# A two-layer transformer trunk on one core: FFN second product of groups 0 to 7 as Strassen's seven block products, with weight block sums on GpSimd

## The reference, cut to what matters

```python
def conv_ffn(x, w_in, conv_w, conv_b, w_out):
    up, gate = jnp.split(x @ w_in, 2, axis=-1)          # x 256x1024, w_in 1024x5632
    up = conv1d_causal_depthwise(up, conv_w) + conv_b   # 3 taps along the tokens
    return (jax.nn.gelu(up) * gate) @ w_out             # hidden 256x2816, w_out 2816x1024
...
x = layer_norm(DEEPNORM_ALPHA * x + conv_ffn(x, ...), ln_g[layer, 1], ln_b[layer, 1])
```

## Time and profile before

| | |
|---|---|
| median of 3 runs | 592.69 us |
| the profiled execution's own time | 593.44 us |
| its span (first to last instruction) | 590.9 us |
| PE busy | 580.6 us (98%) |
| weight loads of PE (beside matmuls) | 473.7 us (80%) |
| VectorE busy | 448.5 us (76%) |
| ScalarE busy | 335.3 us (57%) |
| GpSimd busy | 50.9 us (9%) |
| mean granted TensorE clock | 0.997 |
| DMA | 127.86 MB, mean 216 GB/s |

### The profile page before, as it was taken

How to read it: one execution, slowest core, us unless ns; L and a number is a source line. 1 busy time by engine, 2 the same in 40 slices (tenths; PEclk the granted TensorE clock), 3 DMA queues, 4 the chain that set the end, 5 groups by cost and what they waited for, 6 DMA issues and landing times.

```text
span 590.9 us, 7752 instructions
## 1 busy us (share of the span) xinstructions
PE 580.6 (98%) x2720; PEld 473.7 (80%) x2720; DVE 448.5 (76%) x813; ACT 335.3 (57%) x560; POOL 50.9 (9%) x84
## 2 busy tenths in 40 slices
PE   8999999999999999999999999999999999999995
PEld 6887777788888888888888888887888888888884
DVE  4889995886688777667879796778677888766656
ACT  4767584245566656554545678944556574555530
POOL 5300000400000000000120003132000000000003
PEclk9999999999999999999999999999999999999998
DMA  8997876456668798866456955442965889777511
GB/s 298 297 325 232 273 176 214 132 182 207 202 211 262 252 336 259 262 207 219 154 202 192 333 175 174 136 143 72 311 184 181 252 257 334 243 235 246 179 36 71
DMA packets 95665, 127.86 MB, mean 216 GB/s; under 512 B 13404, under 2 KB 73612, under 8 KB 95628
## 3 DMA queue, kind: packets, MB, share of 16 engines
q1 hardware_dynamic: 94188, 123.19, 65.3%
q0 software_dynamic: 1152, 4.19, 2.0%
q10 hardware_dynamic: 288, 0.00, 0.0%
HBM read 108.23 MB, written 1.05 MB: 185 GB/s over the span
## 4 chain that ended last, share of the span: by engine, by line
PE 95%; DVE 3%; DMA 1%; ACT 0%; issue 0%; SPq 0%; DVEq 0%
PE wide L1288 18%; PE wide L1290 17%; PE wide L1289 17%; PE score L1290 6%; PE score L1288 6%; PE score L1289 6%; PE outb L1290 3%; PE turn L1290 3%; PE outb L1288 3%; PE turn L1288 3%; PE outb L1289 3%; PE turn L1289 3%; DMA xs<-in_x 1%; DVE xT L994 1%; PE turn L1387 1%; PE outb L1413 1%
## 5 line engine op out<-in xcount | busy, mean ns | idle before, releaser
L977 DVE TENSOR_TENSOR w_lo<-raw,w_hi 128x2048 fp32r<-128x2048 f32 (+1 forms) x120 | 210.5, 1776 | 60.5 <-ACT w_hi L790 60.3
L790 ACT ACTIVATE w_hi<-raw 128x2048 fp32r<-128x2048 f32 (+1 forms) x126 | 184.2, 1488 | 92.3 <-PE wide L1290 45.5
L1288 PE MATMUL wide<-w_hi,oT_hi 128*128 128x512 f32 x240 | 95.0, 396 | 0.0
L1290 PE MATMUL wide<-w_hi,oT_lo 128*128 128x512 f32 x240 | 93.5, 390 | 0.0
L1289 PE MATMUL wide<-w_lo,oT_hi 128*128 128x512 f32 x240 | 93.5, 390 | 0.0
L1288 PE MATMUL wide<-w_hi,xT 128*128 128x512 f32 x224 | 89.9, 401 | 0.5 <-DVE xT L994 0.3
L1290 PE MATMUL wide<-w_hi,xT 128*128 128x512 f32 x224 | 87.4, 390 | 0.0
L1289 PE MATMUL wide<-w_lo,xT 128*128 128x512 f32 x224 | 87.3, 390 | 0.0
L1288 PE MATMUL score<-w_hi,xT 128*128 128x512 f32 x160 | 62.2, 389 | 0.0
L1289 PE MATMUL score<-w_lo,xT 128*128 128x512 f32 x160 | 62.2, 389 | 0.0
L1290 PE MATMUL score<-w_hi,xT 128*128 128x512 f32 x160 | 62.2, 389 | 0.0
(11 more groups left out here) (160 smaller groups left out, 837.9 us busy)
## 6 DMA issues: line engine op xcount, KB each, us to landing
raw<-in_ffn_w_in SPq DMA_DIRECT2D x88, 512.0 KB, 5.4
raw<-in_ffn_w_out SPq DMA_DIRECT2D x22, 1024.0 KB, 7.6
kT<-turned SPq DMA_DIRECT2D x104, 128.0 KB, 2.8
raw<-in_a_w_qkv SPq DMA_DIRECT2D x9, 1024.0 KB, 6.8
raw<-in_w_kv_shared SPq DMA_DIRECT2D x8, 1024.0 KB, 7.0
raw<-in_a_w_o SPq DMA_DIRECT2D x4, 1024.0 KB, 6.2
raw<-in_b_w_q SPq DMA_DIRECT2D x4, 1024.0 KB, 5.1
raw<-in_b_w_o SPq DMA_DIRECT2D x4, 1024.0 KB, 5.2
```

Source lines behind the costliest of these rows:

```text
L790: ins = nc.scalar.activation(w_hi[c % RING][:, part], raw[c % RAW_RING][:, part], ACT.Copy)
L977: ins = nc.vector.tensor_tensor(w_lo[c % RING][:, part], raw[c % RAW_RING][:, part], w_hi[c % RING][:, part].bitcast(F32), ALU.subtract)
L1288: nc.tensor.matmul(dst, a_hi, b_hi, start=start, stop=False, skip_group_check=True)
L1290: return nc.tensor.matmul(dst, a_lo, b_hi, start=False, stop=stop, skip_group_check=True)
```

## The change

**Second product of groups 0 to 7** (`FOLDED = 8`). The 2x2 blocks are: hidden, by token tile and feature tile; weights, by feature tile and half of the output columns. Instead of eight block products there are seven, each of one 128x128 stationary operand and 512 moving columns (21 matmuls a group instead of 24), of sums and differences of blocks:
- hidden side: `combine` (DVE) makes five sums into `h_sums` (three instructions), then hi and lo of 5 + 2 tiles.
- weight side, a chunk of 2048 columns becomes 3584: the two plain blocks (`fold_plain_hi` on ACT, `fold_plain_lo` on DVE, 1024 columns), and five sums. GpSimd's `fold_weights` makes the sums (1024, 1024 and 512 columns), ACT their hi parts (1024 and 1536), GpSimd the lo parts (1024 and 1536). These results have one buffer each (`fold_hi`/`fold_lo`, parts a and b).
- the seven products accumulate over the eight groups in seven PSUM banks: four in part A (`fold_a`), three in part B (`fold_b`). So one bank, `side[3]`, is left for the first products of groups 2 to 9, and both token tiles use it in turn.
- after group 7 VectorE adds the seven banks to the residual, 12 instructions of 128x512 (`add_folded`), before groups 8 to 10 use `wide`.

**PE's order** is now, for group i: first product of token tile 0 (24 matmuls), part A of group i-2 (12), first product of token tile 1 (24), part B of group i-2 (9).

**The last group's first product** (`in_features`) has the weights stationary and the 256 tokens moving: 96 matmuls of 256 columns instead of 48 of 512. Its result has the features on the partitions, so its transposes and move fall away (`MOVES = GROUPS - 1`).

**Chunks of groups 8 and 9** of w_out are split by GpSimd (four instructions of 1024 columns a layer). Some buffers change place so that the new ones fit.

The core of the diff:

```diff
-HIDDEN = 4
-MOVE_AHEAD = 6
+FOLDED = 8
...
+        POOL_SPLITS[2 * layer, 1] = ([], [(c + 2 * GROUPS + n, half) for n in range(2) for half in range(2)])
...
+        fold_a = ((1, wide[0]), (0, side[0]), (2, side[2]), (3, side[1]))
+        fold_b = ((6, wide[1]), (5, wide[3]), (4, wide[2]))
...
+            def fold_weights(t):
+                four = quadrants(t)
+                pool.wait_ge(raw_in[raw_slot("fold", t)], raw_count("fold", t))
+                if t:
+                    pool.wait_ge(sum_lo_done, t)
+                nc.gpsimd.tensor_tensor(fold_sums[0].rearrange("p (t n) -> p t n", t=2), four[:, :, 0, :], four[:, :, 1, :],
+                                        ALU.add).then_inc(sums_a_done, 1)
+                if t:
+                    pool.wait_ge(fold_b_lo_done, t)
+                nc.gpsimd.tensor_tensor(fold_sums[1][:, 0:D].rearrange("p (h n) -> p h n", h=2), four[:, 1, :, :], four[:, 0, :, :],
+                                        ALU.subtract)
+                nc.gpsimd.tensor_tensor(fold_sums[1][:, D:D + HALF], four[:, 0, 0, :], four[:, 1, 1, :],
+                                        ALU.add).then_inc(sums_b_done, 1)
+                pool.wait_ge(sum_hi_done, t + 1)
+                nc.gpsimd.tensor_tensor(fold_lo[0][:, CHUNK // 2:CHUNK], fold_sums[0], fold_hi[0][:, CHUNK // 2:CHUNK].bitcast(F32),
+                                        ALU.subtract).then_inc(sum_lo_done, 1)
+                pool.wait_ge(fold_b_hi_done, t + 1)
+                nc.gpsimd.tensor_tensor(fold_lo[1], fold_sums[1], fold_hi[1].bitcast(F32),
+                                        ALU.subtract).then_inc(fold_b_lo_done, 1)
...
+                def out_folded(j, half):
+                    t, b = FOLDED * layer + j, j % 2
+                    if half == 0:
+                        pe.wait_ge(hlo_done, 2 * (GROUPS * layer + j) + 2)
+                        pe.wait_ge(plain_lo_done, t + 1)
...
+                    else:
+                        pe.wait_ge(fold_b_lo_done, t + 1)
+                    for n, (tile, bank) in enumerate(fold_b if half else fold_a):
+                        if half == 0 and n == 2:
+                            pe.wait_ge(sum_lo_done, t + 1)
...
+                for i in range(MOVES):
+                    for st in range(ST):
+                        in_half(i, st)
+                        if i >= 2:
+                            out_folded(i - 2, st)
+                for which in range(2):
+                    in_features(which)
```

More of the change, by code:

```diff
@@ L328, in yoco_trunk @@
             POOL_SPLITS[2 * layer + 1, 0] = ([], [(c + 1, 1), (c + 2, 0)])
-    POOL_PARTS = [part for n in range(2 * LAYERS) for st in range(ST) for parts in POOL_SPLITS.get((n, st), ([], [])) for part in parts]
+    for n in range(2 * LAYERS):
+        for st in range(ST):
+            for parts in POOL_SPLITS.get((n, st), ([], [])):
+                POOL_PARTS += parts
     POOL_CHUNKS = sorted({c for c, _ in POOL_PARTS})
@@ L629, in _ @@
                         else:
[L630 removed]
+                            load("chunk", c, (lambda r: r.rearrange("p (k n) -> p k n", k=4), src))
                         if c == FIRST + 2:
@@ L643, in load_in @@
                     for h in range(2):
-                        load(ffn_chunk(layer, i, h),
+                        load("chunk", in_chunk(layer, i, h),
                              *[(lambda r, w=w: r.rearrange("p (k w n) -> p k w n", k=4, w=2)[:, :, w, :],
@@ L938, in _ @@
+                    if 1 <= i <= FOLDED:
+                        fold_b_hi(i - 1)
+                    if i < GROUPS - 1:
+                        split_hi(in_chunk(layer, i, 1) + RING)
+                make_h_hi(GROUPS - 1)
+                for c in (base + LAYER_CHUNKS, base + LAYER_CHUNKS + 1):
+                    for half in range(2):
+                        split_hi(c, half)
                 if layer + 1 < LAYERS:
@@ new lines, in turn_in @@
+                    dve.wait_ge(*((in_rows_done, u + 1) if st == 0 else (chunk_used, in_chunk(layer, i, 1) + 1)))
+                    if st == 0 and u >= 2:
+                        dve.wait_ge(in_carried, 64 * (u - 1))
+                    into = turned[:, u % 2, :, :].rearrange("p b (j s t) -> p b j s t", j=4, s=ST)
+                    nc.vector.transpose(into[:, :, :, st, :], in_bank(i, st)[:, :].rearrange("p (j f b) -> p b j f", j=4, b=4)
+                                        ).then_inc(in_turned, 1)
@@ L1222, in add_taps, with add_folded @@
+                def add_folded(adds):
+                    for st, half, bank, op, after in adds:
+                        part = xs[:, st, half * HALF:(half + 1) * HALF]
+                        if after:
+                            dve.wait_ge(folded_added, 12 * layer + after)
+                        nc.vector.scalar_tensor_tensor(part, part, 1.0 if after else ALPHA, bank[:, :], ALU.mult,
+                                                       op).then_inc(folded_added, 1)
                 def add_taps(i):
@@ L1260, in _ @@
+                    split_lo(in_chunk(layer, i, 0) + RING)
+                    if i < MOVES:
+                        split_lo(in_chunk(layer, i, 1) + RING)
+                    else:
+                        make_h_lo(i)
+                        for half in range(2):
+                            split_lo(base + LAYER_CHUNKS, half)
+                        if layer + 1 < LAYERS:
+                            split_shared_lo()
                     if (layer, i) == (0, 0):
@@ new lines, in out_product @@
+                    return last
+                for i in range(MOVES):
+                    for st in range(ST):
+                        in_half(i, st)
+                        if i >= 2:
+                            out_folded(i - 2, st)
+                for which in range(2):
+                    in_features(which)
+                for st in range(ST):
+                    for half in range(2):
+                        last = out_product(FOLDED, st, half)
+                last.then_inc(chunk_used, 1)
```

401 lines of the change are left out of this document (253 added, 148 removed).

## The result

| | before | after |
|---|---|---|
| median of the runs, us | 592.76 (592.5 to 593.11, 4 runs) | 694.77 (693.61 to 695.15, 4 runs) |
| ratio, 95% interval | | 1.1717 (1.1697 to 1.1738) |
| span of the profiled execution, us | 590.9 | 692.8 |
| mean granted clock, share of 2.4 GHz | 0.997 | 0.946 |

The change makes the kernel slower by 102 us, 17%. The forecast was 708 us, in a range of 605 to 752.

A forecast was written before the change was run, and what follows sets the result against it. PE's matmuls were taken to bound the kernel. From the profiled 593.4 us, - 10.9 + 1.3 + 115 + 6 + 4 = 708.8, forecast as 708 us against the median of the runs; own range 670 to 752, with most of rival 2 605 to 752.

The forecast's parts named there:

- The mechanism: GpSimd instructions reading SBUF and VectorE's two-input SBUF instructions exclude each other, so in folded groups they only alternate; chance 0.69.
- 48 matmuls taken away: Second product on PE: 3 of 24 matmuls fewer in 8 groups and 2 layers, at 0.227 us each, 10.9 us less.
- 192 of 256 columns for 96 of 512: Last group's first product on PE, both layers: smaller matmuls taken at 0.12 us each, +1.3 us.
- 16 groups longer than 15.6: Folded groups: the alternating chain takes 22.8 us where PE needs 15.6, so 7.2 us of waiting each, +115 us.
- ends of the layers: PE waits some 3 us a layer (+6); GpSimd's splits for groups 8 and 9 push VectorE's chain (+4).
- start of folding, and the clock after the waits: No term in the sum for filling the chain at each layer's start or for a lower PE clock.
- I let both go against the filling of the chain at the start: Both: the first folded group's little lead and the last one's missing sums, taken to cancel against filling the chain.
- the turned bank: Sign in the FFN: PE would wait for the turned bank (`in_turned`) and for GpSimd's lo parts.
- its digits on the page: Sign on the profile page: PE's busy digits at 6 or 7 in the FFN.
- Rival 1: The engines do not exclude each other, or so little that PE stays fed at 15.6 us a group: 589 us; chance 0.14.
- Rival 2: GpSimd waits for VectorE but VectorE never for GpSimd: 17.5 us a group, 620 us, range 595 to 650; chance 0.12.
- Rival 3: PE's clock drops to 1.2 GHz when PE stands still in groups; more than 752 us given chance 0.05.

The follow-up runs named there:

- run 1: The changed kernel with each of GpSimd's five instructions in a folded group replaced by two fills of the same output, sums and low parts left out: 609.45 us.
- run 3: The changed kernel with two more GpSimd additions of 256 columns a group that read SBUF, results unused, after the sums of part B: 706.4 us.
- run 4: The changed kernel with four more GpSimd fills a group after the sums of part B, into buffers that nothing reads then: 694.39 us.
- run 9: The changed kernel with GpSimd's five additions and subtractions in a folded group replaced by copies of their first input: 613.07 us.
- run 7: The changed kernel with ScalarE's copy of group 9's chunk of w_out moved behind group 9's taps: 689.83 us.
- run 10: The kernel of run 2 with ScalarE's copy of group 9's chunk of w_out moved behind group 9's taps: 629.71 us, ratio 1.0623.
- run 11: The kernel of run 1 with ScalarE's copy of group 9's chunk of w_out moved behind group 9's taps: 607.28 us, ratio 1.0243.
- run 2: The changed kernel with all five of GpSimd's instructions in a folded group (three sums, two low parts) done on VectorE: 634.21 us, ratio 1.0697.
- run 12: The kernel of run 11 with group 2's first transpose from PSUM put ahead of group 1's second split on VectorE: 599.79 us, ratio 1.0118.

## Why the prediction was right, and where by luck

**The mechanism held.** The one step that no row of before could show, that VectorE waits for a long GpSimd instruction as GpSimd waits for VectorE, stands in the timeline at three taps and two splits of one group, and runs 1, 3 and 4 give it from both sides: take the reading away and 85 us go, add a little reading and 11.6 come, add writing and nothing comes. The Trainium skill, SBUF — State Buffer, section Who interferes with whom, has the first of the two hold what they share for its whole instruction and the other one fully blocked; the trace agrees (a split of 2.28 us lasted 5.08, to 2.1 us after GpSimd's end), and so does run 9, where GpSimd reads one input (taps of 671 and 788 ns on the mean).

**The terms, one by one.**

| term | forecast | measured |
|---|---|---|
| 48 matmuls taken away | -10.9 | -10.9 by PE's pace, 0.227 us |
| 192 of 256 columns for 96 of 512 | +1.3, 0.12 us apart | +1.2: 0.120 us (95 distances in 11.39 us) |
| 16 groups longer than 15.6 | +115, 22.8 us each | +87, 21.04 us each |
| ends of the layers | +10 | PE's last waits, 9.4 |
| start of folding, and the clock after the waits | 0 | some 15 |
| sum on 593.4 | 708.8 | 695.1 (the profiled execution took 694.58) |

The last line but one is the difference of runs, not a row: run 1's span of 606.6 us is 25.4 above 590.9 - 9.7 = 581.2, of which 18.0 are PE's waits at starts and ends (8.7 + 8.1 + 1.2) and the rest fits its clock (0.986 for 0.997: 0.011 x 607 = 6.7). 25 less the 10 at the ends is 15. It may be carried over to the changed kernel: the eight group distances of each layer come to 165.9 and 169.9 us there and to 125.1 and 125.5 in run 1, 85.2 more, and the spans differ by 86.2.

**The first mis-sized term** is the one that decides: "Alternating, one group takes ... 22.8 us". The chain I followed was the right one, and each of its pieces came out a little shorter: taps with two sums between them 6.4 us for 7.2 (217.69 to 224.07), the part up to the hidden low part 4.1 for 4.3, from there to the end of the second split, with two low parts between, 9.9 for 10.4. The hand-overs, for which I added 0.2, take time off instead: the start of one engine's instruction lies under the end of the other's. 1.75 us less in 16 groups is 28 us.

**The second** is "I let both go against the filling of the chain at the start". They don't cancel: in run 1 PE stands still for 4.7 and 4.5 us at the two starts (8.0 and 9.4 in the changed kernel, where the split ahead of the awaited transpose takes 5.05 us beside GpSimd), and works at 1.2 GHz for 3.4 us after it and after the wait at the end. With the clock this is 15 us, in the other direction. The main term was 28 us too high, and this one, put at nothing, hid half of it: that the forecast of 708 lies only 13 off is luck.

**The ends** came out at 9.4 us for 10, but my reason was half of it. The wait for group 9's chunk carried 2 to 5 us of the time (runs 7, 10, 11); the rest is, by the trace, again a GpSimd instruction beside taps.

**Signs that came out otherwise.** PE waited for the turned bank, as forecast, but hardly for GpSimd's low parts (no matmul did, weight loads for 0.7 us in all); and its digits on the page were 7 to 9 in most of the FFN, not 6 or 7, since matmuls at the lower clock count as busy for longer.

**The rivals.** Rival 1 (no exclusion, 589 us) is dead by the durations, and run 1 shows that its number was wrong too: with nothing shutting VectorE out, the new order alone costs 609. Rival 2 (only GpSimd waits) would leave VectorE's means at 2284 and 480 ns; they are 3513 and 1423. Rival 3 named something real: in the changed kernel and in run 1 the clock falls to 1.2 GHz at every wait of 3.3 us or more. But inside a folded group that is covered by VectorE; it costs only where PE is the bound, at the starts and ends.

**No version beat the kernel before.** The best one that computes everything is 629.7 us (run 10), 6% slower. Even with the sums and low parts left out and both queues mended, 599.8 us stay 1.2% above. The change saves 9.7 us on PE in all, 0.6 a folded group, and that is less than what the vector work needs: 5120 further columns a group, 1.22 + 1.22 + 0.69 + 1.18 + 1.75 = 6.1 us of VectorE in run 2, where a group of PE is 15.6 us long and VectorE, busy 76% of the time before, has some 12 us of other work in it.

## What to carry to other kernels

An idle GpSimd is no free helper for additions in SBUF beside a VectorE that works on two SBUF inputs: count its time (here 2.4 us per 1024 columns, against 1.2 on VectorE itself) as VectorE's, unless it stands beside work from PSUM or beside waits, and even there compare it with VectorE using that wait. Fills by GpSimd did not hold VectorE up. Before taking matmuls away from a bound PE, price what the additions cost on the engine that feeds it, and look at the first and the last group by themselves: here one wait of 4 us at the start of each of two layers, with the clock that came after it, was worth 7.5 us (runs 11 and 12).

## What the runs showed of the hardware

- A GpSimd fill of 1024 columns took 0.955 us (run 1), a copy 1.08 to 1.20 (run 9), an addition or subtraction 2.38 where VectorE did not hold it and up to 3.11 on the mean where it did (changed kernel).
- VectorE is held by a GpSimd instruction that reads one input as well as by one that reads two, and not by one that only writes: the split of 2048 columns took 2275 ns on the mean with fills, 3513 with additions, and taps 671 and 788 ns with copies.
- VectorE's transpose from PSUM beside a reading GpSimd instruction kept its 0.71 us, and that instruction its 2.37.
- Whenever PE had stood still for 3.3 us or more, in the changed kernel and in every run, it was granted 1.2 GHz (0.50), matmuls 0.43 us apart, for 3.4 us in most cases and 6.8 in the stretch shown. Waits of 3.0 us went both ways: in run 11 the clock stayed at 1.00 after the one at the end of layer 0 and fell after the one at the end of layer 1. After waits of 0.9 and 1.4 us (run 12) it stayed at 1.00.
- A matmul of 256 columns followed the last after 0.120 us with its own weight load beside it, one of 512 after 0.227 (changed kernel).
